# A first megabyte of the second expert's second layer in the residual's space, and the halves behind it one place ahead

## The reference

```
mix = (sum_b sigmoid(g_b) * (y_b @ W_branch[b])) @ W_out
h   = LayerNorm(alpha * x + mix)
x   = LayerNorm(alpha * h + MoE(h))    top-4 of 32 clamped-SwiGLU experts
expert(e): clamped_swiglu(h @ w1[e] + b1[e]) @ w2[e] + b2[e]
w1: (32, 1024, 2048), w2: (32, 1024, 1024)
```

## Time and profile before

| what | value |
|---|---|
| median of three runs | 1285.55 us |
| profiled execution, span from first to last instruction | 1282.2 us |
| PE busy | 1242.3 us (97%) |
| DVE busy | 452.2 us (35%) |
| ACT busy | 219.6 us (17%) |
| DMA moved | 458.70 MB, mean 358 GB/s over the span |
| granted TensorE clock, mean | 0.998 |

### The profile page before, as it was taken

The page is one execution under the profiler, slowest core; times in us unless marked ns, Lnnn a source line. Parts: engine busy times, 40 slices in busy tenths (PEclk is TensorE's granted clock), DMA queues, the critical chain, the costliest instruction groups (busy, mean ns, idle before and its releaser), DMA issues.

```text
span 1282.2 us, 14909 instructions
## 1 busy us (share of the span) xinstructions
PE 1242.3 (97%) x6126; PEld 643.6 (50%) x6126; DVE 452.2 (35%) x914; ACT 219.6 (17%) x430; POOL 3.5 (0%) x17
## 2 busy tenths in 40 slices
PE   9999999999999999999999999999998999899996
PEld 8888888998873343333333333333323333333332
DVE  5999924556342512121321213212121312122123
ACT  1722124231040110101111010110101010110102
POOL 0000000000000000000000000000000000000000
PEclk9999999999999999999999999999999999999999
DMA  9534344336979999999999999999999999999996
GB/s 380 204 134 152 109 154 160 114 110 223 424 280 408 429 432 426 435 431 429 433 429 434 432 429 433 429 434 432 429 433 429 434 430 430 433 428 428 428 424 260
DMA packets 31486, 458.70 MB, mean 358 GB/s; under 512 B 4785, under 2 KB 5169, under 8 KB 9426
## 3 DMA queue, kind: packets, MB, share of 16 engines
q1 hardware_dynamic: 27728, 453.00, 84.2%
q10 hardware_dynamic: 3714, 5.07, 1.2%
HBM read 457.01 MB, written 1.05 MB: 357 GB/s over the span
## 4 chain that ended last, share of the span: by engine, by line
PE 74%; DMA 16%; DVE 7%; ACT 1%; issue 1%; DVEq 0%; SPq 0%; POOL 0%; POOLq 0%
PE banks L1333 20%; PE banks L910 15%; PE banks L1369 14%; DMA store<-in_moe_w 13%; PE banks L1341 4%; PE banks L924 4%; DMA store<-in_w_last 3%; PE banks L1160 2%; PE banks L1185 2%; DVE store L2057 2%; PE banks L1440 2%; PE banks L1249 2%; PE banks L1351 1%; DVE store L2054 1%; DVE store L2051 1%; DVE store L2056 1%
## 5 line engine op out<-in xcount | busy, mean ns | idle before, releaser
L1333 PE MATMUL banks<-store 128*64 128x512 f32 x1536 | 342.6, 595 | 16.7 <-DMA store<-in_moe_w 16.6
L1333 PEld LDWEIGHTS banks<-store 128*64 128x64 f32 x1536 | 109.4, 137 | 231.9 <-issue 205.7
L1369 PE MATMUL banks<-store 128*64 128x512 f32 x952 | 210.9, 595 | 0.0
L910 PE MATMUL banks<-store 128*128 128x256 f32 x896 | 196.8, 380 | 0.0
L910 PEld LDWEIGHTS banks<-store 128*128 128x128 f32 x896 | 169.3, 190 | 26.4 <-issue 3.9
L2051 DVE TENSOR_SCALAR store<-banks 128x512 f32<-128x512 f32 x32 | 22.1, 692 | 428.8 <-PE banks L1341 428.8
L1369 PEld LDWEIGHTS banks<-store 128*64 128x64 f32 x952 | 65.9, 137 | 142.8 <-issue 120.1
L1341 PE MATMUL banks<-store 128*64 128x512 f32 x512 | 116.8, 598 | 0.4 <-DMA store<-in_moe_w 0.4
L2065 DVE COPY store<-banks 64x512 f32<-64x512 f32 x30 | 20.8, 694 | 203.3 <-PE banks L1369 203.3
L789 ACT ACTIVATE store<-store 128x512 f32<-128x512 f32 x28 | 17.6, 630 | 431.0 <-DVE store L2051 431.0
L1341 PEld LDWEIGHTS banks<-store 128*64 128x64 f32 x512 | 34.3, 136 | 70.1 <-issue 67.7
(11 more groups left out here) (380 smaller groups left out, 842.3 us busy)
## 6 DMA issues: line engine op xcount, KB each, us to landing
store<-in_moe_w SPq DMA_DIRECT2D x72, 4096.0 KB, 30.3
store<-in_moe_w SPq DMA_DIRECT2D x36, 2048.0 KB, 14.7
store<-in_w_in SPq DMA_DIRECT2D x30, 1024.0 KB, 4.8
store<-in_moe_w SPq DMA_DIRECT2D x18, 1024.0 KB, 9.3
store<-in_w_branch SPq DMA_DIRECT2D x8, 1024.0 KB, 4.8
store<-in_w_out SPq DMA_DIRECT2D x4, 1024.0 KB, 6.0
store<-in_w_last SPq DMA_DIRECT2D x4, 1024.0 KB, 34.8
store<-in_w_first SPq DMA_DIRECT2D x4, 256.0 KB, 4.3
```

Of the source, the lines that this page charges most:

```text
L910: last = mm(b[:, j * SEQ:(j + 1) * SEQ], w[:, k, j * P:j * P + P], xT[:, k, :], start=k == 0, stop=k == KD - 1)
L1333: last = mm(bank[into[i]][64 * ct:64 * ct + 64, :], xg[:, 2 * c + kk, col:col + CAP], w[:, kk, i * FF + ct * 512:i * FF + ct * 512 + 512], ...
L1369: last = mm(bank[4][64 * dh:64 * dh + 64, :], actT[:, j, 64 * fh:64 * fh + 64], w[j][:, 512 * dh:512 * dh + 512], start=(fh, j) == (0, 0), ...
```

## The change

In SP's program the first half of unit 10 (the GUEST) goes into the space of `x_res`, in two parts, each when `x_hat` of that half of the rows is done. Every half behind it, in the list SHIFTED (units 10 to 17 without 13), goes into the place of the half in front of it (`shifted`), and is asked for when that one has been used. The loop for units 18 to 29 waits for the last user of its place (`last_user`). TensorE takes its weights from these places, through `in_parts`. `normed` moves behind the use of the guest and writes `y_acc`. The gather's chunks 6 and 7 come after the first unit; their semaphores and PSUM places are adapted. Three small transfers share one semaphore (`rw_in`).

```diff
@@ -64,6 +64,8 @@
 HOME = 3
 BIAS_PAIR = 11
 APART = 3 * NU - 1
+GUEST = 2 * NDBL
+SHIFTED = [(m, i) for m in range(2 * NDBL, 3 * NU) if m != 2 * NDBL + HOME for i in range(2)]
 
 
 VR = {}
...
@@ -330,9 +332,9 @@
 
             if k in (1, 2):
                 return bank[5 + k][:, 0:P]
-            if k == 5:
-                return bank[4][:, 0:P]
-            return bank[2 + k // 4][:, (k % 4) * P:(k % 4 + 1) * P]
+            if k in (3, 5):
+                return bank[(5, 4)[k // 5]][:, 0:P]
+            return bank[3 if k == 4 else 2][:, (k % 4) * P:(k % 4 + 1) * P]
 
...
@@ -367,6 +369,15 @@
                 return first_unit_at
             lo = place(m // 2) + UNIT * (m % 2)
             return store[:, lo:lo + UNIT]
+
+        def shifted(m, i):
+
+            m, i = SHIFTED[SHIFTED.index((m, i)) - 1]
+            return unit_at(m)[:, SLOT * i:SLOT * i + SLOT]
+
+        def last_user(m):
+
+            return max(u for u, _ in SHIFTED[SHIFTED.index((m, 0)):][:3]) if (m, 0) in SHIFTED else m
 
         LAST = (NE - 1) * NU
         TAIL = [(NE - 2, c) for c in range(NW1)] + [(NE - 1, c) for c in range(NW1)]
@@ -442,32 +453,45 @@
             load_part(8, 1).then_inc(unit_landed[4], 16)
             load_part(9, 0).then_inc(unit_landed[5], 16)
             sp.dma_start(spare[:, D:2 * D], unit_source(2, NU - 1)[:, SLOT + D:UNIT]).then_inc(S["apart_landed"], 16)
-            for i in range(2):
-                for part in (slice(0, FF), slice(FF, 2 * FF)) if i == 0 else (slice(0, 2 * FF),):
-                    sp.wait_ge(S["half_used"], part.stop // FF + i)
-                    e, c = HEAD[2 * NDBL + i]
-                    sp.dma_start(unit_at(2 * NDBL + i)[:, part], unit_source(e, c)[:, part]).then_inc(S["half_landed"], 16)
-                sp.wait_ge(S["expert_chunk_used"], i + 1)
-                load_part(2 * NDBL + i, 1).then_inc(double_landed[NU // 2 - 1], 16)
-            sp.wait_ge(S["ln_used"], 2)
-            sp.dma_start(spare[:, 0:D], unit_source(2, NU - 1)[:, SLOT:SLOT + D]).then_inc(S["apart_landed"], 16)
-            for m in range(2 * NU, 3 * NU):
-                if m == 2 * NDBL + HOME:
-                    continue
-                if 2 * NDBL + NW1 <= m < APART:
-                    sp.wait_ge(S["half_used"], m - 2 * NDBL)
-                    sp.dma_start(unit_at(m)[:, 0:SLOT], unit_source(2, m - 2 * NU)[:, 0:SLOT]).then_inc(S["apart_landed"], 16)
-                    sp.wait_ge(S["expert_chunk_used"], m - 2 * NDBL + 1)
-                    sp.dma_start(unit_at(m)[:, SLOT:UNIT], unit_source(2, m - 2 * NU)[:, SLOT:UNIT]).then_inc(double_landed[(m // 2 - NU // 2) % NU], 16)
-                    continue
-                sp.wait_ge(S["expert_chunk_used"], m - 2 * NDBL + 1)
-                if m == APART:
-                    sp.dma_start(unit_at(m)[:, 0:SLOT], unit_source(2, NU - 1)[:, 0:SLOT]).then_inc(double_landed[NU - 1], 16)
-                else:
-                    load_half(m)
+            for half in range(2):
+                sp.wait_ge(S["x_hat_ready"], 4 * half + 4)
+                sp.dma_start(x_res[:, half, :], unit_source(*HEAD[GUEST])[:, D * half:D * half + D]).then_inc(S["half_landed"], 16)
+
+            def load_shifted(m, i):
+
+                e, c = HEAD[m] if m < 2 * NU else (2, m - 2 * NU)
+                return sp.dma_start(shifted(m, i), unit_source(e, c)[:, SLOT * i:SLOT * i + SLOT])
+
+            for j in range(2):
+                sp.wait_ge(S["half_used"], j + 1)
+                sp.dma_start(shifted(GUEST, 1)[:, D * j:D * j + D], unit_source(*HEAD[GUEST])[:, SLOT + D * j:SLOT + D * j + D])\
+                    .then_inc(double_landed[NU // 2 - 1] if j else S["half_landed"], 16)
+            sp.wait_ge(S["expert_chunk_used"], 1)
+            load_shifted(11, 0).then_inc(S["half_landed"], 16)
+            sp.wait_ge(S["half_used"], 3)
+            load_shifted(11, 1).then_inc(double_landed[2], 16)
+            sp.wait_ge(S["expert_chunk_used"], 2)
+            load_shifted(12, 0).then_inc(S["half_landed"], 16)
+            sp.wait_ge(S["expert_chunk_used"], 3)
+            load_shifted(12, 1).then_inc(double_landed[3], 16)
+            load_shifted(14, 0).then_inc(S["apart_landed"], 16)
+            sp.wait_ge(S["half_used"], 4)
+            load_shifted(14, 1).then_inc(double_landed[4], 16)
+            sp.wait_ge(S["expert_chunk_used"], 5)
+            load_shifted(15, 0).then_inc(S["apart_landed"], 16)
+            sp.wait_ge(S["half_used"], 5)
+            load_shifted(15, 1).then_inc(double_landed[4], 16)
+            sp.wait_ge(S["expert_chunk_used"], 6)
+            load_shifted(16, 0).then_inc(S["apart_landed"], 16)
+            sp.wait_ge(S["half_used"], 6)
+            load_shifted(16, 1).then_inc(S["apart_landed"], 16)
+            sp.wait_ge(S["expert_chunk_used"], 7)
+            load_shifted(17, 0).then_inc(double_landed[5], 16)
+            sp.wait_ge(S["expert_chunk_used"], 8)
+            sp.dma_start(unit_at(APART)[:, 0:D], unit_source(2, NU - 1)[:, SLOT:SLOT + D]).then_inc(double_landed[5], 16)
 
             for m in range(3 * NU, 5 * NU):
-                sp.wait_ge(S["expert_chunk_used"], m - 2 * NDBL + 1)
+                sp.wait_ge(S["expert_chunk_used"], last_user(m - 2 * NDBL) + 1)
                 d = NU // 2 + (m // 2 - NU // 2 ^ 1)
                 n = 2 * d + m % 2
...
@@ -770,9 +794,12 @@
 
             def gathered(g, first=False):
 
-                act.wait_ge(S["xg_first"], g + 1)
                 for k in range(KD):
-                    if k == 4:
+                    if first and k in (0, 2):
+                        act.wait_ge(S["xg_early"], k // 2 + 1)
+                    elif k == (4 if first else 0):
+                        act.wait_ge(S["xg_first"], g + 1)
+                    elif k == (6 if first else 4):
                         act.wait_ge(S["xg_psum"], g + 1)
                     src = first_place(k) if first else bank[2 + k // 4][:, (k % 4) * P:(k % 4 + 1) * P]
...
@@ -1230,15 +1257,13 @@
             pe.wait_ge(S["sel_ready"], 1)
             for k in range(3):
                 pe.wait_ge(S["x_hat_ready"], 5 + k)
-                first_gather(1, (k,))
+                last = first_gather(1, (k,))
+                if k == 1:
+                    last.then_inc(S["xg_early"], 1)
             first_gather(0, (3,))
             pe.wait_ge(S["x_hat_ready"], 8)
-            first_gather(1, (3,)).then_inc(S["xg_first"], 1)
-            first_gather(1, (4, 5))
-            for k in (6, 7):
-                first_gather(0, (k,))
-                last = first_gather(1, (k,))
-            last.then_inc(S["xg_psum"], 1)
+            first_gather(1, (3,)).then_inc(S["xg_early"], 1)
+            first_gather(1, (4, 5)).then_inc(S["xg_first"], 1)
...
@@ -1263,7 +1288,10 @@
                 if c % 2 == 0:
                     pe.wait_ge(double_landed[c // 2], 32)
                 if c == NW1:
-                    pe.wait_ge(S["half_landed"], 48)
+                    pe.wait_ge(S["half_landed"], 16 * 5)
+                    return (x_res.rearrange("p a b -> p (a b)"), shifted(GUEST, 1))
+                if c > NW1:
+                    return (shifted(GUEST + 1, 0), shifted(GUEST + 1, 1))
                 return head_at(1, c)
 
             def last_but_one_unit(c):
...
@@ -1311,6 +1339,10 @@
                 else:
                     pe.wait_ge(double_landed[c // 2], NPAIR * 16 + 16)
                 return unit_at((NE - 3) * NU + c)
+
+            def in_parts(v, n):
+
+                return [a[:, n * j:n * j + n] for a in (v if isinstance(v, tuple) else (v,)) for j in range(a.shape[-1] // n)]
 
...
-                    w = unit(c).rearrange("p (k n) -> p k n", k=2)
+                    w = in_parts(unit(c), SLOT)
                     if c < NW1 - 1:
...
-                    whole = unit(c)
-                    w = [whole[:, D * j:D * j + D] for j in range(4)]
-                    if last_apart and c == NU - 1:
-                        w[2:] = [spare[:, D * j:D * j + D] for j in range(2)]
+                    w = in_parts(unit(c), D)
                     fh = c - NW1
...
                     mm(bank[COMB_BANK[i]][:, :], wTd[0:NE + 1, half, :], b2_all[0:NE + 1, 512 * dh:512 * dh + 512], start=True, stop=True).then_inc(S["comb_psum"], 1)
 
-            first_layer(first_unit, 0, 0, returned=((0, 0), (0, 1), (1, 1)))
+            first_layer(first_unit, 0, 0, cs=(0,), returned=((0, 0), (0, 1)))
+            for k in (6, 7):
+                first_gather(0, (k,))
+                last = first_gather(1, (k,))
+            last.then_inc(S["xg_psum"], 1)
+            first_layer(first_unit, 0, 0, cs=(1, 2, 3), returned=((1, 1),))
             bias(1, (2, 3))
...
@@ -1487,18 +1521,23 @@
                 if not final:
                     second_layer(second_unit, p * 2 + 2, p * 2 + 3)
 
-            expert_two_unit = pair_unit(0, 0, 1, 32)
-
             def third_unit(c):
 
+                m = 2 * NU + c
```

(46 more changed lines are left out.)

2 lines of the change are left out of this document (removed).

## The result

The changed kernel takes 1290.26 us (median of five runs, 1289.63 to 1290.64) against 1285.55 us: 4.7 us slower, ratio 1.0039 with a 95% interval of 1.0027 to 1.0052. The forecast was 1290.05 us.

What follows compares the result with a forecast made beforehand. The prediction took one DMA stream from 381 us on as the bound: 6.7 us of new holes less 2.2 us gained is 4.5 us, so 1285.55 + 4.5 = 1290.05 us, range 1287.9 to 1291.8 us.

Steps and rivals of the forecast that it cites:

- The bound: From 381 us on one DMA stream without a hole sets the end; TensorE's lead is eaten up by 800 us.
- The hole at 380 us goes: At 379 to 382 us the guest fills the stream's last hole entirely, 1.96 us idle by share or 2.54 us of transfer.
- The gain is 2.2 us: Filling the hole at 379 to 382 us puts the stream ahead by 2.2 us, between 1.96 and 2.45 us.
- My in-hand sum for 395.81 us: At 395.81 us the new queue ends at 400.3 against 398.1, so 2.2 us are in hand and no hole comes.
- Three holes: Later waits of the 2 MB loop's third, fourth and fifth requests leave holes of 0.8, 2.67 and 3.17 us, 6.7 us together.
- The sum, 4.5 us: Over the whole stream, holes of 6.7 us against 2.2 us gained make the end 4.5 us later.
- The check by one landing: The fifth 2 MB request's place in the stream moves from landing at 443.0 to 440.28 + 7.2 = 447.5 us, +4.5 us.
- Cost at nothing: Smaller requests, ScalarE's later copies of chunks 6 and 7 and the two moved VectorE multiplies were costed at nothing.
- Advance kept: Rival: the 1 MB shift lasts to the end, later waits find enough in the queue; 1283.35 us, chance 0.08.
- no effect: Rival: TensorE sets the end and both edits of the stream are lost; 1285.55 us, chance 0.05.
- one hole more: Rival: the queue runs dry already at 412.58 us, about 1.5 us more; 1291.55 us, chance 0.07.
- What was foretold of the trace: Full share at 379 to 382 us, holes near 426, 431 to 434, 439 to 442, first-layer idle 41.4 to about 46 us.

Runs made afterwards that it cites:

- the waits alone: The kernel before, with only the third to fifth and seventh to ninth requests of its 2 MB loop waiting for the later unit counts: 1289.99 us, ratio 1.0040.
- Splitting: The kernel before, with units 18 to 29 each asked for as two 1 MB halves at the old times: 1285.69 us, ratio 1.0003.
- the halves kernel: The changed kernel with units 20 to 22 and 24 to 27 asked for in 1 MB halves as places come free, sixth unit before the fifth's second half: 1285.46 us.
- the later fifth request: The changed kernel with the fifth request of the 2 MB loop waiting for count 16 instead of 15: 1295.08 us, ratio 1.0079.
- the late one: The halves kernel with the guest waiting until unit 0's first half is used: 1285.08 us; with the first three 4 MB requests also split: 1284.07 us.

## Why the prediction was right, step by step

**The bound.** One DMA stream from 381 us sets the end, and TensorE has time to spare. Right: 4.65 us put into the stream at 441 us came out as 4.8, and the chain's last link kept its length (37.02, 37.05).

**The hole at 380 us goes.** Right: 1.241 MB where 0.196 had been, 2.44 us of transfer.

**The gain is 2.2 us.** Wrong, the term of the sum that was mis-sized. By the earlier trace rows the second 2 MB request had landed at 428.3; in the trace of after it is issued at 417.00, 0.99 us later, and lands after 11.3 us, at 428.3 again. Allowing for the 0.99 the gain is 1.0 us there, not 2.2, and 0.65 if only what this execution was behind before the guest is allowed for. 1.2 us had been lost at 390 to 404 us (371 instead of 407 GB/s). My in-hand sum for 395.81 us (2.2 us, no hole) was right in that the stream did not stop, and blind to the lower rate.

**Three holes.** The second and third right in place and size: they lie between requests 7.57 and 8.07 us apart in both traces (425.63, 433.20, 441.27), each with 4.90 us to move. The first was put at 0.8 us. By landings it is nothing: the third request lands at 433.2, 4.9 us after the second. By bytes there is a dip of 1.0 us at 425 to 427 (221 GB/s in two microseconds) that the next ones partly make good.

**The sum, 4.5 us.** The measured loss is 4.7. Two terms were off and partly made up for each other (gain at least 1.2 too high, first hole 0.8 too high by landings), so that the sum of the terms comes out close is in part luck. The mechanism does not hang on it: the waits alone, without any gain and with two holes, end as late, so neither term matters. Once a hole ends, the stream's place is issue plus landing of the request behind it. The check by one landing in the prediction (440.28 + 7.2 against 443.0) leaves both terms out and is the better sum; it lacks only TensorE's 0.34 us below.

**Cost at nothing.** Splitting (1285.69 us by itself), normed rows, list and gather (1285.78 us together with the guest): right within what can be told. From the first request for unit 10 to the last one before the 2 MB loop, SP's timelines have 16 requests after and 14 before: the change adds two and not the three of the prediction. The sum has no term for them. TensorE's part was not quite nothing: the eight gather passes between two units take 1.16 us and not 0.99, and put all later units back by 0.34 us.

**Advance kept (rival, 0.08)** needed more in hand than there was, and did not come even in the halves kernel, which has none of the three holes; **no effect (TensorE sets the end, 0.05)** is out by the later fifth request; **one hole more (0.07)** did not come. What was foretold of the trace came true in place, 0.99 us later. The idle time of the first-layer line was misread: 41.4 us counts matmuls and weight loads, whose waits overlap, so that it grew to 53.9 us and not to 46, while the matmuls' own grew from 16.6 to 21.3 us, by the 4.7 us that were lost. These waits begin near 656 us and not after 800 (the chain's first link is a request of 627.82 that lands after 31.36 us).

## What to carry to other kernels

Where one queue sets the end, find the last request that meets it empty: here everything that was won or lost before that request was worth nothing, and its issue time passed to the end one to one. Before a buffer is re-cut, write down for every place who uses it last and which request waits for that; shifting by half a slot under requests of whole slots makes every one of them wait for the next user. Extra space pays only if all thin places behind it have more in hand than the advance; here a margin of 2.2 us read from landings did not keep the stream full. And before idle time of a line is added up, see whether it counts matmuls and weight loads together.

## What the runs showed of the hardware that was not expected

A full DMA share does not mean a full rate: with the early guest the share over 390 to 404 us was 0.99 to 1.00 at 358 to 372 GB/s, with the late one 1.01 at 403 to 405, with the same requests there. The reason is open. Twelve more requests in a full queue changed 428 to 422 GB/s in 430 to 470 us, and the time by 0.5 us, which is not told from noise (1.1 us). What a landing in an empty queue takes beyond the transfer at 428 GB/s was the same for 0.5 MB and 2 MB: 3.5 - 1.22 and 7.2 - 4.90, both 2.3 us.
